# Offsets of 32 bytes between TensorE's two operands in a hybrid attention, convolution and expert block

## The chip, the cores and the metric

The kernel runs on one core of one Trainium2 chip. The metric is the device time of one execution in microseconds (us); the number given for a kernel is the median of its runs. Lower is better.

## The reference

One decoder layer on 256 tokens of width 1024, all in float32. `xn` and `hn` are RMS-normalised activations.

```
h = x + W_out( sig(g_conv) * ConformerConv(xn) + sig(g_attn) * DilatedAttn(xn) )
y = h + PEER(RMSNorm(h))

PEER, for each token and each of 8 heads:
  q = hn @ w_q                      # two halves of 128
  s = q . sub_keys                  # 128 scores per half; top 16 of each
  best 16 of the 16 x 16 sums -> experts e = i1 * 128 + i2, gate = softmax
  y += sum_e gelu(u_tab[e] . hn) * gate_e * v_tab[e]
```

There are 128 x 128 = 16,384 experts. The kernel does not gather rows: it computes the product of all of `u_tab` with all tokens, multiplies by a gate that is zero for experts not picked, and multiplies the result with all of `v_tab`.

## The kernel before

**Tiles.** Every weight arrives from HBM as a tile of 128 partitions x 1024 float32 (512 KB), through a ring of four slots, `raw`. There are 76 front tiles (projections, attention and convolution output, mixer, `w_q`), 128 tiles of `u_tab` (the key stage) and 128 of `v_tab` (the value stage). To keep float32 accuracy with the faster `float32r` matmuls, each tile is split: ScalarE writes the rounded copy `hi` (`split_hi`, L327), then VectorE or GpSimd writes the rest `lo = raw - hi` (`split_lo`, L344). Which of the two does it depends on the slot (`by_dve`): of four value tiles two go to each. Every product is then three matmuls, hi x hi, hi x lo and lo x hi, for each unit of 128 of the contraction.

**Operands.** TensorE has a stationary operand (128 columns, loaded by LDWEIGHTS, engine row PEld) and a moving operand (256 or 512 columns, streamed by MATMUL, engine row PE). In the front and key stages the stationary one is a unit of the weight tile (`hi`, `lo`), the moving one the 256 tokens. The tokens' own split parts are in `nrm` (normalised tokens, merged branches; interleaved `[k][hi, lo][256]`) or, for some jobs, in `rounded` (`xg_hi`, `xg_lo` for GLU and `w_q`; `o_hi`, `o_lo` for attention; `cu_hi`, `cu_lo` for convolution). `product` (matmul at L1222) issues these, 24 matmuls of 256 columns for a tile of the front or of the first half of the key stage. `v_tile_of` (L1322) does the v projection with `nrm` stationary and the weights moving.

**Key stage, second half.** 64 tiles go through `wide_tile`: for each of 8 units one matmul of 512 columns (`hi` with both token parts, L1478) and one of 256 (`lo` with the high part, L1480). Between them stand the matmuls of the gates (L1492, 16 to a group, one group to two tiles).

**Value stage.** `v_tile` (L1537) has the activations stationary and the value tile moving: 12 matmuls of 512 columns for a tile. The activations are in `act`; `a_split` (ScalarE, L662) and `low_part` (VectorE, L1148) write a tile's two parts into four slots of `nrm`, which the key stage no longer needs. In the first 64 value tiles VectorE also does gate work, and gate matmuls stand between tiles as before; in the last 64 there is none. The last tiles are finished at L1563 and the output is stored.

**Order.** The order on each engine is written out by hand and tied with semaphores; `pe_step` counts TensorE's steps and frees slots of `hi` and `raw`, `lo_ready` tells that a `lo` is there, `a_hi` and `a_lo` that the activations' parts are.

**Addresses.** The tensors lie one behind the other in a partition in the order of the code, every start rounded up to 32 bytes. `raw` starts at byte 16,512, a multiple of 64; `hi`, `lo` and `nrm` follow 16,384 bytes apart, and units, parts and slots are steps of 512 bytes or more, so each operand out of them starts at a multiple of 64 bytes. `rounded` starts at byte 188,448, which is 32 above a multiple of 64; so do `resid`, `qk` and `prob`, while `ident` and `act` start at multiples of 64.

The loads of the front and both halves, cut:

```
def load(src, base, it, j):
    if not (isinstance(it, int) and base + 4 * it + j < RING):
        wait_lo(sp, base - 4, it, j)
    sp.dma_start(raw[:, slot_of(base, j), :], src).then_inc(raw_in[slot_of(base, j)], 16)
```

## Time and profile before

| | before |
|---|---|
| median of 3 runs | 1028.22 us (1027.71 to 1028.9) |
| the profiled execution's own time | 1028.21 us |
| its span, first to last instruction | 1026.4 us |
| PE busy | 1020.2 us (99%) |
| VectorE, ScalarE, GpSimd busy | 811.2, 523.8, 543.4 us |
| granted TensorE clock | 1.00 (the higher level) in every slice |
| read from HBM | 180.33 MB, 179 GB/s |

The span is cut by the kernel's stages at about 225 us (mixer ends, `w_q`), 269 us (key stage), 450 us (its second half), 653 us (value stage), 850 us (its second half) and 1018 us (last sums and stores). PE's busy time says only that matmuls are always in flight: they overlap, so the pace is read from the distance between starts, not from their lengths.

### The profile page before, as it was taken

The numbers are of one execution on the slowest core, as the hardware profiler recorded it, in microseconds if no ns is written. First come the engines' busy times: TensorE is split into PE (matmuls) and PEld (weight loads), VectorE is DVE, ScalarE is ACT, GpSimd is POOL, SyncE is SP. The second block draws the span as 40 slices with busy tenths as digits, with TensorE's granted clock in tenths as the row PEclk, the third lists the DMA queues.
The fourth block names the chain that finished last, engine by engine and source line by source line (L and its number), as shares of the span: only waits on it lengthen the run. The fifth ranks groups of instructions, "written<-read, shape, count | busy, mean of one in ns | idle before, by whom it ended". The sixth has DMA issues, their size and how long they took to land.

```text
span 1026.4 us, 21174 instructions
## 1 busy us (share of the span) xinstructions
PE 1020.2 (99%) x7326; PEld 910.8 (89%) x7326; DVE 811.2 (79%) x1347; ACT 523.8 (51%) x852; POOL 543.4 (53%) x230
## 2 busy tenths in 40 slices
PE   9999999999999999999999999999999999999998
PEld 9998999999999999998888888777777778888887
DVE  6999674758799999466666666899999997677664
ACT  6553877544544444545555555544444445454553
POOL 4554455556689999864433334434443334444442
PEclk9999999999999999999999999999999999999999
DMA  6684445554455555555545555554555555655652
GB/s 242 226 289 133 138 144 182 175 178 160 146 188 182 169 192 173 184 171 174 168 163 170 177 172 176 173 176 163 165 174 172 174 173 184 201 188 186 202 191 96
DMA packets 52618, 181.93 MB, mean 177 GB/s; under 512 B 5943, under 2 KB 9155, under 8 KB 52452
## 3 DMA queue, kind: packets, MB, share of 16 engines
q1 hardware_dynamic: 52292, 181.16, 53.7%
q8 instruction: 24, 0.39, 0.2%
q10 hardware_dynamic: 288, 0.27, 0.1%
q14 instruction: 14, 0.11, 0.0%
HBM read 180.33 MB, written 3.43 MB: 179 GB/s over the span
## 4 chain that ended last, share of the span: by engine, by line
PE 96%; ACT 1%; DVE 1%; issue 1%; POOL 1%; ACTq 0%; DVEq 0%; POOLq 0%
PE bank L1222 35%; PE bank L1537 33%; PE bank L1478 12%; PE bank L1480 6%; PE bank L1492 3%; PE bank L1322 2%; PE bank L1237 1%; PE bank L1454 1%; DVE nrm L1148 1%; ACT hi L327 1%; PE bank L1246 1%; PE bank L1563 1%; PE bank L1338 0%; POOL lo L344 0%; PE bank L1361 0%
## 5 line engine op out<-in xcount | busy, mean ns | idle before, releaser
L344 POOL TENSOR_TENSOR lo<-raw,hi 128x1024 fp32r<-128x1024 f32 x216 | 540.5, 2512 | 469.0 <-ACT hi L327 468.7
L327 ACT CAST hi<-raw 128x1024 fp32r<-128x1024 f32 x332 | 347.5, 1048 | 225.0 <-PE bank L1537 191.0
L1222 PE MATMUL bank<-nrm,hi 128*128 128x256 f32 x1600 | 290.2, 284 | 0.0
L1537 PE MATMUL bank<-hi,nrm 128*128 128x512 f32 x1008 | 281.0, 395 | 1.4 <-DVE nrm L1148 1.4
L1222 PEld LDWEIGHTS bank<-nrm,hi 128*128 128x128 f32 x1600 | 249.2, 192 | 2.1 <-issue 1.3
L1222 PE MATMUL bank<-nrm,lo 128*128 128x256 f32 x800 | 226.4, 283 | 0.0
L1537 PEld LDWEIGHTS bank<-hi,nrm 128*128 128x128 f32 x1008 | 184.3, 188 | 44.9 <-DVE nrm L1148 10.0
L1148 DVE TENSOR_TENSOR nrm<-act,nrm 128x256 fp32r<-128x256 f32 x128 | 180.8, 1415 | 50.0 <-ACT nrm L662 50.0
L1478 PE MATMUL bank<-nrm,hi 128*128 128x512 f32 x512 | 181.8, 399 | 0.0
L344 DVE TENSOR_TENSOR lo<-raw,hi 128x1024 fp32r<-128x1024 f32 x116 | 148.8, 1283 | 40.2 <-ACT hi L327 40.1
L1537 PE MATMUL bank<-lo,nrm 128*128 128x512 f32 x504 | 155.8, 390 | 0.0
L1222 PEld LDWEIGHTS bank<-nrm,lo 128*128 128x128 f32 x800 | 153.3, 192 | 0.0
L1480 PE MATMUL bank<-nrm,lo 128*128 128x256 f32 x512 | 142.0, 277 | 0.0
L1478 PEld LDWEIGHTS bank<-nrm,hi 128*128 128x128 f32 x512 | 96.0, 188 | 20.9
L1537 PEld LDWEIGHTS bank<-lo,nrm 128*128 128x128 f32 x504 | 94.6, 188 | 20.3
L1480 PEld LDWEIGHTS bank<-nrm,lo 128*128 128x128 f32 x512 | 96.1, 188 | 0.0
L1222 PE MATMUL bank<-rounded,hi 128*128 128x256 f32 x496 | 89.1, 282 | 0.5 <-POOL lo L344 0.5
L1222 PEld LDWEIGHTS bank<-rounded,hi 128*128 128x128 f32 x496 | 76.2, 189 | 1.6 <-issue 0.8
L630 ACT ACTIVATE act<-bank 128x256 f32 x64 | 24.6, 384 | 93.9 <-PE bank L1222 93.8
L651 ACT COPY half_sum<-bank 128x256 f32<-128x256 f32 x64 | 23.8, 372 | 93.2 <-PE bank L1480 93.2
L1222 PE MATMUL bank<-rounded,lo 128*128 128x256 f32 x248 | 69.6, 281 | 0.0
L1154 DVE TENSOR_TENSOR half_sum<-bank,half_sum 128x256 f32<-128x256 f32 x64 | 27.0, 421 | 38.1 <-ACT half_sum L651 38.1
(188 smaller groups left out, 988.9 us busy)
## 6 DMA issues: line engine op xcount, KB each, us to landing
raw<-u_tiles SPq DMA_DIRECT2D x128, 512.0 KB, 3.3
raw<-v_tiles SPq DMA_DIRECT2D x128, 512.0 KB, 3.3
raw<-front SPq DMA_DIRECT2D x76, 512.0 KB, 3.9
toeplitz<-bias_row SPq DMA_DIRECT2D x6, 384.0 KB, 7.4
bias<-toeplitz SPq DMA_DIRECT2D x12, 128.0 KB, 3.6
resid<-x_t SPq DMA_DIRECT2D x2, 512.0 KB, 4.8
qk<-sub_keys SPq DMA_DIRECT2D x1, 1024.0 KB, 7.5
y<-act SPq DMA_DIRECT2D x3, 256.0 KB, 2.0
```

Source lines behind the costliest of these rows:

```text
L327: act_e.copy(hi[:, s, :], raw[:, s, :]).then_inc(hi_ready, 1)
L344: eng.tensor_tensor(lo[:, s, :], raw[:, s, :], hi[:, s, :].bitcast(F32), ALU.subtract)\
L630: a.activation(act[:, it * 4 + (base_i + j), :], bank[4 + j % 2][:, 0:T], ACT.Gelu).then_inc(gelu_done, 1)
L651: a.copy(half_sum[:, j % 2, :], bank[4 + j % 2][:, T:2 * T]).then_inc(crossed, 1)
L1148: dve.tensor_tensor(nrm_lo[:, s, :], act[:, it * 4 + (base_i + j), :], nrm_hi[:, s, :].bitcast(F32), ALU.subtract).then_inc(a_lo, 1)
L1154: dve.tensor_tensor(half_sum[:, j % 2, :], bank[4 + j % 2][:, 0:T], half_sum[:, j % 2, :], ALU.add)\
L1222: ins = pe.matmul(dst, w_[:, s, u * P:(u + 1) * P], x_[:, k, :], start=first and i == 0 and p_ == 0, stop=last and i == n - 1 and p_ == 2)
L1322: ins = pe.matmul(b[:, c * T:(c + 1) * T], x_[:, k, c * P:(c + 1) * P], w_[:, n % RING, 2 * m * P:2 * (m + 1) * P], start=k == 0 and c == ...
L1478: pe.matmul(b[:, :], hi[:, j, unit], nrm[:, k, :, :].rearrange("p a t -> p (a t)"), start=k == 0, stop=False, skip_group_check=True)
L1480: ins = pe.matmul(b[:, 0:T], lo[:, j, unit], nrm_hi[:, k, :], start=False, stop=k == KB - 1, skip_group_check=True)
L1492: ins = pe.matmul(bank[6 + g][:, q * HALF:(q + 1) * HALF], ohA[:, g, q // PAIR, :, q % PAIR], ohB[:, g, q // PAIR, i, :, q % PAIR], start= ...
L1537: ins = pe.matmul(bank[2 * c + half][:, :], a_[:, j, c * P:(c + 1) * P], v_[:, j, half * 512:(half + 1) * 512], start=False, stop=False, s ...
```

## The change

`SHIFT` is 8 float32, 32 bytes. Tokens (`nrm`) now start 32 bytes into their space, so that in the front and key stages the moving operand out of `nrm` starts 32 bytes above a multiple of 64, the stationary one at a multiple of 64. In the value stage the activations' parts get a view of the same space that is not shifted (`act_hi`, `act_lo`), and the value tiles' parts are written 32 bytes into their slots (`value_hi`, `value_lo`); for that the slots of `hi` and `lo` are 1040 instead of 1024 elements long. Front and key tiles still start at their slots' beginning. GpSimd's second loop over `split_lo` is cut in three, since tile 203 is the last key tile and tile 204 the first value tile. `gains` moves behind `rounded`: with 32 bytes more ahead of it and these 32 bytes less, `rounded` keeps its place 32 above a multiple of 64. `act` moves from a multiple of 64 to 32 above one. No instruction is added to or removed from a stage.

```
--- before.py
+++ after.py
@@ -42,6 +42,8 @@
 N_U = N_V = NK
 RING = 4
 LEAD = 3
+
+SHIFT = 8
 CHUNK_STEPS = PH // 2 + 9
 TOP_TILES = 48
 EXP_TILE = 52
@@ -173,10 +175,15 @@
 
 
         raw = sb("raw", [P, RING, D])
-        hi = sb("hi", [P, RING, D], F32R)
-        lo = sb("lo", [P, RING, D], F32R)
-        nrm = sb("nrm", [P, KB, 2, T], F32R)
+        hi_space = sb("hi_space", [P, RING, D + 2 * SHIFT], F32R)
+        lo_space = sb("lo_space", [P, RING, D + 2 * SHIFT], F32R)
+        hi, lo = hi_space[:, :, 0:D], lo_space[:, :, 0:D]
+        value_hi, value_lo = hi_space[:, :, SHIFT:SHIFT + D], lo_space[:, :, SHIFT:SHIFT + D]
+        norm_space = sb("norm_space", [P, KB * 2 * T + SHIFT], F32R)
+        nrm = norm_space[:, SHIFT:].rearrange("p (k a t) -> p k a t", a=2, t=T)
         nrm_hi, nrm_lo = nrm[:, :, 0, :], nrm[:, :, 1, :]
+        picked_acts = norm_space[:, 0:RING * 2 * T].rearrange("p (k a t) -> p k a t", a=2, t=T)
+        act_hi, act_lo = picked_acts[:, :, 0, :], picked_acts[:, :, 1, :]
         ident = sb("ident", [P, P])
         iota = sb("iota", [P, TOPK])
 
@@ -191,7 +198,6 @@
 
         kmask = tmp("kmask", [P, 2 * HEADS - 2])
         ksel = tmp("ksel", [HEADS, AB, P])
-        gains = tmp("gains", [P, 1])
         oneh = tmp("oneh", [BUCKETS + 1, GROUPS, BW])
         sq = tmp("sq", [P, KB, T])
         rs = tmp("rs", [P, 2, 512])
@@ -208,6 +214,7 @@
         cu_hi, cu_lo = rounded[:, 0:CB, :], rounded[:, CB:2 * CB, :]
         o_hi, o_lo = rounded[:, 2 * CB:2 * CB + AB, :], rounded[:, 2 * CB + AB:, :]
         xg_hi, xg_lo = rounded[:, 0:KB, :], rounded[:, KB:2 * KB, :]
+        gains = tmp("gains", [P, 1])
         stat = tmp("stat", [P, 16, TC * HEADS])
 
         resid = tmp("resid", [P, KB, T])
@@ -318,13 +325,17 @@
         def wait_raw(eng, base, it, j):
             eng.wait_ge(raw_in[slot_of(base, j)], uses(base, it, j) * 16)
 
+        def is_value(base, it, j):
+
+            return base + j >= V0 or isinstance(it, int) and base + 4 * it + j >= V0
+
         def split_hi(act_e, base, it, j):
 
             s = slot_of(base, j)
             wait_raw(act_e, base, it, j)
             if not (isinstance(it, int) and base + 4 * it + j < RING):
                 wait(act_e, pe_step, step_of(base - 4, it, j))
-            act_e.copy(hi[:, s, :], raw[:, s, :]).then_inc(hi_ready, 1)
+            act_e.copy((value_hi if is_value(base, it, j) else hi)[:, s, :], raw[:, s, :]).then_inc(hi_ready, 1)
 
         def by_dve(base, j):
 
@@ -341,7 +352,8 @@
 
             s = slot_of(base, j)
             eng.wait_ge(hi_ready, it * 4 + (base + j + 1))
-            eng.tensor_tensor(lo[:, s, :], raw[:, s, :], hi[:, s, :].bitcast(F32), ALU.subtract)\
+            hi_, lo_ = (value_hi, value_lo) if is_value(base, it, j) else (hi, lo)
+            eng.tensor_tensor(lo_[:, s, :], raw[:, s, :], hi_[:, s, :].bitcast(F32), ALU.subtract)\
                .then_inc(lo_ready[s], 1)
 
         def whole(k, round_):
@@ -445,11 +457,18 @@
             pool.wait_ge(normed, 2 * KB)
             pool.iota(iota_nk[:, :, :], pattern=[[1, NK], [0, PAIR]], base=0, channel_multiplier=0,
                       allow_small_or_imprecise_dtypes=True).then_inc(const, 1)
-            for base, tiles in ((U0 + LEAD, HALF), (G_SHARED, N_U + N_V - RING - HALF)):
+            for base, tiles in ((U0 + LEAD, HALF), (G_SHARED, HALF - RING)):
                 with pool.Fori(0, tiles // RING) as it:
                     for j in range(RING):
                         if not by_dve(base, j):
                             split_lo(pool, base, it, j)
+            for j in range(RING):
+                if not by_dve(G_SHARED, j):
+                    split_lo(pool, G_SHARED, HALF // RING - 1, j)
+            with pool.Fori(0, (N_V - RING) // RING) as it:
+                for j in range(RING):
+                    if not by_dve(V0 + LEAD, j):
+                        split_lo(pool, V0 + LEAD, it, j)
 
         @block.scalar
         def _(a):
@@ -659,7 +678,7 @@
             def a_split(base_i, it, j):
 
                 wait(a, pe_step, it * 4 + (S_V + base_i + j - 3))
-                a.copy(nrm_hi[:, (base_i + j) % RING, :], act[:, it * 4 + (base_i + j), :]).then_inc(a_hi, 1)
+                a.copy(act_hi[:, (base_i + j) % RING, :], act[:, it * 4 + (base_i + j), :]).then_inc(a_hi, 1)
 
             def key_round(it, first=False, last=False):
                 for j in range(RING):
@@ -1145,7 +1164,7 @@
 
                 dve.wait_ge(a_hi, it * 4 + (base_i + j + 1))
                 s = (base_i + j) % RING
-                dve.tensor_tensor(nrm_lo[:, s, :], act[:, it * 4 + (base_i + j), :], nrm_hi[:, s, :].bitcast(F32),
+                dve.tensor_tensor(act_lo[:, s, :], act[:, it * 4 + (base_i + j), :], act_hi[:, s, :].bitcast(F32),
                                   ALU.subtract).then_inc(a_lo, 1)
 
             def add_halves(it, j):
@@ -1530,8 +1549,8 @@
                 wait_lo(pe, V0 + base_i, it, j)
                 pe.wait_ge(a_hi, it * 4 + (base_i + j + 1))
                 for c in range(TC):
-                    for a_, v_ in ((nrm_hi, hi), (nrm_hi, lo), (nrm_lo, hi)):
-                        if c == 0 and a_ is nrm_lo:
+                    for a_, v_ in ((act_hi, value_hi), (act_hi, value_lo), (act_lo, value_hi)):
+                        if c == 0 and a_ is act_lo:
                             pe.wait_ge(a_lo, it * 4 + (base_i + j + 1))
                         for half in range(2):
                             ins = pe.matmul(bank[2 * c + half][:, :], a_[:, j, c * P:(c + 1) * P],
@@ -1559,9 +1578,9 @@
                     wait_lo(pe, V0 + N_V - RING, 0, j)
                     pe.wait_ge(a_hi, N_V - RING + j + 1)
                     pe.wait_ge(a_lo, N_V - RING + j + 1)
-                    for a_, v_ in ((nrm_hi, hi), (nrm_hi, lo), (nrm_lo, hi)):
+                    for a_, v_ in ((act_hi, value_hi), (act_hi, value_lo), (act_lo, value_hi)):
                         ins = pe.matmul(bank[b][:, :], a_[:, j, c * P:(c + 1) * P], v_[:, j, cols],
-                                        start=False, stop=j == RING - 1 and a_ is nrm_lo, skip_group_check=True)
+                                        start=False, stop=j == RING - 1 and a_ is act_lo, skip_group_check=True)
                 ins.then_inc(y_bank, 1)
```

## Rows read from the trace of the kernel before

**Rows 1.** The page: span, busy time, chain by engine and line.

```profile
span 1026.4 us, 21174 instructions
...
PE 1020.2 (99%) x7326; PEld 910.8 (89%) x7326; DVE 811.2 (79%) x1347; ACT 523.8 (51%) x852; POOL 543.4 (53%) x230
...
PE 96%; ACT 1%; DVE 1%; issue 1%; POOL 1%; ACTq 0%; DVEq 0%; POOLq 0%
```

**Rows 2.** The chain in order of time: start us, length us, instructions.

```profile
122.93 1.98 ACT prob L497 x8
...
159.87 39.89 PE bank L1222 x336
...
221.42 3.57 PE bank L1443 x32
225.00 37.02 PE bank L1222 x312
262.02 7.14 PE bank L1454 x64
269.16 172.85 PE bank L1222 x1440
...
849.86 168.04 PE bank L1537 x740
```

**Rows 3.** Timeline of PE in the front, three stretches: start us, length us.

```profile
28.68 0.40 PE L1222 MATMUL bank<-rounded,hi 128*128 128x256 f32 x2
...
29.39 0.40 PE L1222 MATMUL bank<-rounded,hi 128*128 128x256 f32 x2
...
32.33 0.40 PE L1222 MATMUL bank<-rounded,hi 128*128 128x256 f32 x2
...
34.49 0.40 PE L1222 MATMUL bank<-rounded,hi 128*128 128x256 f32 x2
...
161.32 0.40 PE L1222 MATMUL bank<-rounded,hi 128*128 128x256 f32 x2
...
188.07 0.40 PE L1222 MATMUL bank<-nrm,hi 128*128 128x256 f32 x2
```

**Rows 4.** The chain in order of time, second half of the key stage.

```profile
601.37 0.50 PE bank L1492 x16
...
607.50 0.50 PE bank L1492 x16
```

**Rows 5.** Timeline of PE, second half of the key stage.

```profile
461.06 0.40 PE L1478 MATMUL bank<-nrm,hi 128*128 128x512 f32 x1
...
462.45 0.40 PE L1478 MATMUL bank<-nrm,hi 128*128 128x512 f32 x1
```

**Rows 6.** Timeline of all engines, first half of the value stage.

```profile
753.72 1.06 ACT L327 CAST hi<-raw 128x1024 fp32r<-128x1024 f32 x1 [2.08 <-PE bank L1537]
...
754.86 2.52 POOL L344 TENSOR_TENSOR lo<-raw,hi 128x1024 fp32r<-128x1024 f32 x1 [3.63 <-ACT hi L327]
755.04 2.62 DVE L1148 TENSOR_TENSOR nrm<-act,nrm 128x256 fp32r<-128x256 f32 x1
...
757.71 0.77 PEld L1537 LDWEIGHTS bank<-hi,nrm 128*128 128x128 f32 x4 [0.23 <-DVE nrm L1148]
757.75 1.17 PE L1537 MATMUL bank<-hi,nrm 128*128 128x512 f32 x4
...
759.88 1.06 ACT L327 CAST hi<-raw 128x1024 fp32r<-128x1024 f32 x1 [2.07 <-PE bank L1537]
```

**Rows 7.** Waits, 653 to 850 us: total us, times, longest.

```profile
POOL lo L344 <- ACT hi L327: 117.2, 33, 3.7
...
PEld bank L1537 <- DVE nrm L1148: 9.0, 32, 0.9
```

**Rows 8.** Groups by line and shape: busy us, mean ns of one.

```profile
L1154 DVE TENSOR_TENSOR half_sum<-bank,half_sum 128x256 f32<-128x256 f32 x64 | 27.0, 421 | 38.1 <-ACT half_sum L651 38.1
...
L979 DVE TENSOR_TENSOR prob<-bank,rs 128x256 f32<-128x256 f32 x16 | 6.5, 418 | 10.3 <-PE bank L1222 10.3
```

More of the change, by code:

```diff
@@ L44 @@
 LEAD = 3
+SHIFT = 8
 CHUNK_STEPS = PH // 2 + 9
@@ L175, in hybrid_block @@
         raw = sb("raw", [P, RING, D])
-        hi = sb("hi", [P, RING, D], F32R)
-        lo = sb("lo", [P, RING, D], F32R)
-        nrm = sb("nrm", [P, KB, 2, T], F32R)
+        hi_space = sb("hi_space", [P, RING, D + 2 * SHIFT], F32R)
+        lo_space = sb("lo_space", [P, RING, D + 2 * SHIFT], F32R)
+        hi, lo = hi_space[:, :, 0:D], lo_space[:, :, 0:D]
+        value_hi, value_lo = hi_space[:, :, SHIFT:SHIFT + D], lo_space[:, :, SHIFT:SHIFT + D]
+        norm_space = sb("norm_space", [P, KB * 2 * T + SHIFT], F32R)
+        nrm = norm_space[:, SHIFT:].rearrange("p (k a t) -> p k a t", a=2, t=T)
         nrm_hi, nrm_lo = nrm[:, :, 0, :], nrm[:, :, 1, :]
+        picked_acts = norm_space[:, 0:RING * 2 * T].rearrange("p (k a t) -> p k a t", a=2, t=T)
+        act_hi, act_lo = picked_acts[:, :, 0, :], picked_acts[:, :, 1, :]
         ident = sb("ident", [P, P])
@@ L193, in hybrid_block @@
         ksel = tmp("ksel", [HEADS, AB, P])
-        gains = tmp("gains", [P, 1])
         oneh = tmp("oneh", [BUCKETS + 1, GROUPS, BW])
@@ L210, in hybrid_block @@
         xg_hi, xg_lo = rounded[:, 0:KB, :], rounded[:, KB:2 * KB, :]
+        gains = tmp("gains", [P, 1])
         stat = tmp("stat", [P, 16, TC * HEADS])
@@ L319, in wait_raw, with is_value @@
             eng.wait_ge(raw_in[slot_of(base, j)], uses(base, it, j) * 16)
+        def is_value(base, it, j):
+            return base + j >= V0 or isinstance(it, int) and base + 4 * it + j >= V0
         def split_hi(act_e, base, it, j):
@@ L326, in split_hi @@
                 wait(act_e, pe_step, step_of(base - 4, it, j))
-            act_e.copy(hi[:, s, :], raw[:, s, :]).then_inc(hi_ready, 1)
+            act_e.copy((value_hi if is_value(base, it, j) else hi)[:, s, :], raw[:, s, :]).then_inc(hi_ready, 1)
         def by_dve(base, j):
@@ L343, in split_lo @@
             eng.wait_ge(hi_ready, it * 4 + (base + j + 1))
-            eng.tensor_tensor(lo[:, s, :], raw[:, s, :], hi[:, s, :].bitcast(F32), ALU.subtract)\
+            hi_, lo_ = (value_hi, value_lo) if is_value(base, it, j) else (hi, lo)
+            eng.tensor_tensor(lo_[:, s, :], raw[:, s, :], hi_[:, s, :].bitcast(F32), ALU.subtract)\
                .then_inc(lo_ready[s], 1)
@@ L447, in _ @@
                       allow_small_or_imprecise_dtypes=True).then_inc(const, 1)
-            for base, tiles in ((U0 + LEAD, HALF), (G_SHARED, N_U + N_V - RING - HALF)):
+            for base, tiles in ((U0 + LEAD, HALF), (G_SHARED, HALF - RING)):
                 with pool.Fori(0, tiles // RING) as it:
@@ L452, in _ @@
                             split_lo(pool, base, it, j)
+            for j in range(RING):
+                if not by_dve(G_SHARED, j):
+                    split_lo(pool, G_SHARED, HALF // RING - 1, j)
+            with pool.Fori(0, (N_V - RING) // RING) as it:
+                for j in range(RING):
+                    if not by_dve(V0 + LEAD, j):
+                        split_lo(pool, V0 + LEAD, it, j)
         @block.scalar
@@ L1532, in v_tile @@
                 for c in range(TC):
-                    for a_, v_ in ((nrm_hi, hi), (nrm_hi, lo), (nrm_lo, hi)):
-                        if c == 0 and a_ is nrm_lo:
+                    for a_, v_ in ((act_hi, value_hi), (act_hi, value_lo), (act_lo, value_hi)):
+                        if c == 0 and a_ is act_lo:
                             pe.wait_ge(a_lo, it * 4 + (base_i + j + 1))
@@ L1561, in _ @@
                     pe.wait_ge(a_lo, N_V - RING + j + 1)
-                    for a_, v_ in ((nrm_hi, hi), (nrm_hi, lo), (nrm_lo, hi)):
+                    for a_, v_ in ((act_hi, value_hi), (act_hi, value_lo), (act_lo, value_hi)):
                         ins = pe.matmul(bank[b][:, :], a_[:, j, c * P:(c + 1) * P], v_[:, j, cols],
-                                        start=False, stop=j == RING - 1 and a_ is nrm_lo, skip_group_check=True)
+                                        start=False, stop=j == RING - 1 and a_ is act_lo, skip_group_check=True)
                 ins.then_inc(y_bank, 1)
```

4 lines of the change are left out of this document (2 added, 2 removed).

## The prediction

> **What bounds the kernel.** I read the page first: PE is busy for 1020.2 of 1026.4 us, and 96% of the chain that ended last is PE [rows 1]. No other engine ends more than 1% of it. So the time is the number of matmuls times their pace, and the question is what a 32-byte offset does to the pace. Busy time can't tell, since matmuls overlap; the chain in order of time can. In the first half of the key stage 1440 matmuls of 256 columns take 172.85 us, 120.0 ns each, with no wait between them. In the second half of the value stage 740 matmuls of 512 columns take 168.04 us, 227.1 ns, or 226.7 without the wait of 0.3 us at their start [rows 2]. The clock is at 2.4 GHz throughout, so these are 288 and 544 cycles: 32 more than columns in both. Those 32 cycles per matmul, whatever the number of columns, are the only thing that the change can touch. With some 5,100 matmuls out of `nrm` they are about 68 us of the time.
>
> **A comparison the kernel already holds.** Jobs at the same line, of the same size, take their moving operand either from `nrm` (a multiple of 64 bytes, like the weights) or from `rounded` (32 above one, while the weights are at 0). This is just the relation that the change gives to `nrm`. The `w_q` tiles, from `rounded`: 312 matmuls in 37.02 us, 118.65 ns [rows 2]. Attention and convolution, from `rounded`: 240 matmuls between 159.87, where the chain's piece starts, and 188.07, where the first `nrm` matmul starts [rows 2, 3]; 28.20 / 240 is 117.5 ns, with a restart at its beginning that makes the pace itself about 117.1. The other 96 of that piece of 336, mixer tiles from `nrm`, take the rest, 159.87 + 39.89 - 188.07 = 11.69 us, 121.8 ns with the end of the group. But a third stretch of `rounded`, the GLU tile after the bias rows, has 18 matmuls from 32.33 to 34.49: 120.0 ns. The tile before the bias rows had 6 from 28.68 to 29.39, 118.3 ns [rows 3]. So at an offset of 0 the pace is 120.0 wherever I look, and at 32 it settles, according to how the group was entered, on 117.1, 118.65 or 120.0. The gain of the offset is 0 to 2.9 ns a matmul. By number of matmuls (240 at 117.1, some 500 at 118.65, one or two tiles at 120.0) the middle one is the commonest; I take 118.65, a gain of 1.35 ns.
>
> **The parts of the change.**
>
> 1. *Key stage, first half.* 64 tiles x 24 = 1536 matmuls of 256 columns, all on the path. 1536 x 1.35 = 2.1 us; bounds 0 and 1536 x 2.9 = 4.5.
>
> 2. *Front tiles out of `nrm`.* 12 q/k, 16 gate and 8 mixer tiles at L1222 and 6 v tiles at L1322 are 42 x 24 = 1008 matmuls. Not all are on the path: from 122.93 on, for some 12 us, the chain runs through ScalarE, its exponentials first [rows 2], which is about 100 matmuls' time. So 900 count: 1.2 us; bounds 0 and 2.6. These are short groups between other work, which must be entered anew each time.
>
> 3. *Key stage, second half.* A pair of 512 and 256 columns takes 348 ns (four from 461.06 to 462.45 [rows 5]), 67 cycles above its 768 columns, again some 32 for each. There is no wait: 16 pairs of 348 ns and a gate group of 0.50 us make 6.07 of the 6.13 us between two gate groups [rows 4]. 1024 matmuls x 1.35 = 1.4 us; but two lengths alternate here, no row shows them at an offset of 32, and I take 1.0; bounds 0 and 3.0.
>
> 4. *Value stage, second half.* The two operands change roles: activations stationary at 0, values moving at 32. 768 matmuls of 512 columns. As the surplus of 32 cycles is the same for 512 as for 256 columns, I carry the gain over: 1.0 us; bounds 0 and 2.2.
>
> 5. *Value stage, first half.* Here a faster PE isn't worth its whole gain. VectorE's `low_part` starts at 755.04 and needs 2.62 us, because it stands until GpSimd's subtraction, begun at 754.86, is over (2.52 us); PE's weight load then ends a wait of 0.23 us, at 757.71. The next `split_hi` starts at 759.88, when PE has finished that tile, and 759.88 - 753.72 = 6.16 us is the period of two tiles [rows 6]. So this is a closed loop: ScalarE 1.06, GpSimd 2.52, VectorE's rest about 0.3, and 2.13 us of PE, from 757.75 to 759.88. PE is in it with 8 of the 24 matmuls. The wait shows in all periods: 32 times, 9.0 us in all [rows 7]. The gain is 256 matmuls x 1.35 = 0.35 us, and the other 512 only make PE wait longer. Upper bound: 256 x 2.9 = 0.7. If the loop were broken it would be three times as much.
>
> 6. *Splits and copies at a new offset.* `split_hi` and `split_lo` write value parts at 32 from a source at 0, and `act` moves by 32. VectorE's rows at both offsets agree: 256 columns to `prob`, at 32, take 418 ns, to `half_sum`, at 0, 421 [rows 8]. I take 0, for ScalarE too, since `split_hi` waits for PE in any case (2.08 us before it [rows 6]). GpSimd has no row at 32, see the rivals. In the second half of the value stage GpSimd waits for most of its time, so an increase of less than a microsecond there is hidden.
>
> 7. *GpSimd's loop in three pieces* issues the same subtractions: it has 117.2 us of waits in 33 pieces in the stage that follows [rows 7], 3.6 us each, which hide some more branches. If they fell into the loop of part 5 it would be once, well under 1 us. The DMAs write the same addresses of `raw`, and nothing new is queued on SP. The move of `gains` leaves `rounded` at 32, so GLU, attention, convolution and `w_q` keep their relation: 0. Their entry, though, can change, by at most the 1.5 ns between two of the paces above for 744 matmuls, 1.1 us either way.
>
> Sum: 2.1 + 1.2 + 1.0 + 1.0 + 0.35 = 5.65 us off the profiled execution's 1028.21 us (1.8 us more than its span, and equal to the median of 1028.22 within 0.01), so 1022.5 us. With all at the best pace seen: 4.5 + 2.6 + 3.0 + 2.2 + 0.7 = 13.0, so 1015.2. With all at 120.0: 1028.2.
>
> A page speaks against the whole gain. Beside the rows of [rows 2, 3], where equal matmuls run at 117.1 to 120.0 ns, stands the rule of the Trainium skill, "SBUF — State Buffer", section "Who interferes with whom": TensorE has two independent read ports, one for the moving operand and one for LDWEIGHTS, and never waits on anyone. If so, no placement of one against the other can matter, and the time stays 1028.2. The trace bears that out only for true float32 matmuls: 32 transposing ones with `ident` at 0 and `resid` at 32 take 3.57 us, 64 with both at 32 take 7.14 us, 111.6 ns in both cases [rows 2].
>
> **The rivals.**
>
> *The offset isn't what makes `rounded` faster.* `rounded` lies 120 KB above the weights, with its high and low parts 8 KB apart instead of interleaved. If one of these made the difference, `nrm` at 32 would stay at 120.0: 1028.2 us. For it: one stretch of `rounded` ran at 120.0 [rows 3], and the float32 rows don't know the offset [rows 2]. Against: 552 or more matmuls did run faster, and no stretch from `nrm` did. The same time comes out if the long groups happen to settle on 120.0.
>
> *All stages settle on the fast pace*, as attention and convolution did for 28 us: 1015 to 1019 us. For it: the pace once taken is held for whole groups, and the first half of the key stage is one group of 1536, so that its whole term is won or lost at its entry. Against: 312 matmuls of `w_q`, just ahead of it and the closest in form, held 118.65.
>
> *The 32 cycles are mostly a collision that the offset removes*, and `rounded` is held up by something else. Then the gain could be several times larger: at the shortest distances inside these groups, about 115 ns, some 5 ns x 4,500 is 22 us, 1006. No stretch kept such a pace; small.
>
> *GpSimd gets slower on value tiles (the other side).* Its subtraction of value tiles now reads `raw` at 0 and `hi` at 32 and writes at 32. It is in the loop of part 5, so each 0.1 us more costs 32 x 0.1 = 3.2 us, and VectorE, shut out meanwhile, passes it on to PE in full. From 0.18 us more (7% of 2.52) it outweighs the 5.65 us; with 0.4 us it is 1028.2 + 12.8 - 5.65 = 1035. For it: nothing in the trace shows GpSimd at mixed offsets. Against: VectorE's equal rows at both [rows 8].
>
> **How the numbers follow.** Gain as forecast, 3 to 9 us: 0.45. Fast pace nearly everywhere, 9 to 14 us: 0.18. More than the rows show: 0.07. No effect beyond 2 us: 0.21. Slower through GpSimd or a worse pace: 0.09. This measurement tells apart changes of about 0.2%, 2 us. Forecast 1022.5. The range of 1014.5 to 1028.8 holds the first two cases, and most of the no-effect one, about 0.82. The likeliest case alone has 1019 to 1025. Faster 0.70, same 0.21, slower 0.09.
>
> **What would show it right or wrong.** In the chain the piece of 1440 matmuls at L1222 shortens from 172.85 us to about 170.9 (at 117.1 ns: 168.6), the 740 at L1537 from 168.0 to about 167. The period of the wide tiles goes from 6.13 to about 6.10, the period in the first half of the value stage from 6.16 to 6.15 with a longer wait of PE for VectorE. ScalarE, VectorE and GpSimd keep their means for L327, L344 and L1148. If the pace is 120.0 everywhere the offset was not the cause; if L344 on GpSimd is above 2.6 us the other side is right; if the value stage moves and the key stage doesn't, roles or lengths of the operands matter and my carrying over from 256 to 512 columns was wrong.

## The result: slower by 0.4%, and the profile after

The changed kernel takes 1032.22 us, the kernel before 1028.04 in the same comparison (6 runs each): ratio 1.004, 95% interval [1.0029, 1.0051]. I had forecast 1022.5 us, 0.55% faster.

The page of the changed kernel still shows a kernel of matmuls:

```profile
span 1030.6 us, 21171 instructions
...
PE 1024.4 (99%) x7326; PEld 911.5 (88%) x7326; DVE 808.2 (78%) x1347; ACT 523.2 (51%) x852; POOL 551.0 (53%) x230
```

Its chain in order of time (start us, length us, instructions) answers to [rows 2]; L1241 is the L1222 of before, L1556 the L1537:

```profile
224.43 36.95 PE bank L1241 x312
...
268.51 170.63 PE bank L1241 x1440
...
848.78 173.14 PE bank L1556 x740
```

The first half of the key stage did what I forecast: 1440 matmuls in 170.63 instead of 172.85 us, 118.5 ns instead of 120.0. The second half of the value stage did the opposite: 740 matmuls in 173.14 instead of 168.04 us, 234.0 instead of 227.1 ns with the wait at their start.

The first gate group of each stage marks its beginning, and gate group 64 the end of the mixed part of the value stage. Timeline of PE, before:

```profile
454.01 0.66 PE L1492 MATMUL bank<-ohB,ohA 128*128 128x64 f16 x16
...
650.27 0.66 PE L1492 MATMUL bank<-ohB,ohA 128*128 128x64 f16 x16
...
842.32 0.66 PE L1492 MATMUL bank<-ohB,ohA 128*128 128x64 f16 x16
```

and after:

```profile
451.01 0.66 PE L1511 MATMUL bank<-ohB,ohA 128*128 128x64 f16 x16
...
648.44 0.66 PE L1511 MATMUL bank<-ohB,ohA 128*128 128x64 f16 x16
...
841.30 0.66 PE L1511 MATMUL bank<-ohB,ohA 128*128 128x64 f16 x16
```

| stage | before us | after us | difference | forecast |
|---|---|---|---|---|
| front, up to 269.16 / 268.51 | 269.16 | 268.51 | -0.65 | -1.2 |
| key stage, first half | 184.85 | 182.50 | -2.35 | -2.1 |
| key stage, second half | 196.26 | 197.43 | +1.17 | -1.0 |
| value stage, first half | 192.05 | 192.86 | +0.81 | -0.35 |
| value stage, second half and end | 184.1 | 189.3 | +5.2 | -1.0 |
| sum | 1026.4 | 1030.6 | +4.2 | -5.65 |

So most of the loss is in matmuls of 512 columns, and the question is what made them slower: the offset itself, the roles of the two operands in the value stage, or the longer slots that the offset needed.

### The profile page after: what moved, and what is told of

The parts are those of the page before. It is cut to its first block, busy times and chain, and to the rows that moved or that the text cites. A ratio compares the mean times of both kernels' runs of the same rounds, so it can differ in the third digit from the quotient of the medians.

```text
span 1030.6 us, 21171 instructions
## 1 busy us (share of the span) xinstructions
PE 1024.4 (99%) x7326; PEld 911.5 (88%) x7326; DVE 808.2 (78%) x1347; ACT 523.2 (51%) x852; POOL 551.0 (53%) x230
## 4 chain that ended last, share of the span: by engine, by line
PE 96%; ACT 2%; DVE 1%; issue 1%; POOL 1%; ACTq 0%; DVEq 0%; POOLq 0%
PE bank L1241 34%; PE bank L1556 34%; PE bank L1497 12%; PE bank L1499 6%; PE bank L1511 3%; PE bank L1341 2%; PE bank L1256 1%; PE bank L1473 1%; DVE norm_space L1167 1%; ACT hi_space L338 1%; PE bank L1265 1%; PE bank L1582 1%; PE bank L1357 0%; POOL lo_space L356 0%; PE bank L1380 0%
## 5 line engine op out<-in xcount | busy, mean ns | idle before, releaser
L356 POOL TENSOR_TENSOR lo_space<-raw,hi_space 128x1024 fp32r<-128x1024 f32 x216 | 548.1, 2548 | 465.1 <-ACT hi_space L338 464.5
L338 ACT CAST hi_space<-raw 128x1024 fp32r<-128x1024 f32 x332 | 346.7, 1045 | 229.8 <-PE bank L1556 197.0
L1241 PE MATMUL bank<-norm_space,hi_space 128*128 128x256 f32 x1600 | 286.6, 282 | 0.0
L1556 PE MATMUL bank<-hi_space,norm_space 128*128 128x512 f32 x1008 | 284.2, 398 | 1.1 <-DVE norm_space L1167 1.1
L1241 PEld LDWEIGHTS bank<-norm_space,hi_space 128*128 128x128 f32 x1600 | 245.2, 188 | 2.2 <-issue 1.5
L1556 PEld LDWEIGHTS bank<-hi_space,norm_space 128*128 128x128 f32 x1008 | 186.7, 188 | 45.3 <-DVE norm_space L1167 2.4
L1241 PE MATMUL bank<-norm_space,lo_space 128*128 128x256 f32 x800 | 224.4, 280 | 0.0
L1497 PE MATMUL bank<-norm_space,hi_space 128*128 128x512 f32 x512 | 183.0, 398 | 0.0
L1556 PE MATMUL bank<-lo_space,norm_space 128*128 128x512 f32 x504 | 158.3, 395 | 0.0
L1241 PEld LDWEIGHTS bank<-norm_space,lo_space 128*128 128x128 f32 x800 | 151.0, 189 | 0.0
L1499 PE MATMUL bank<-norm_space,lo_space 128*128 128x256 f32 x512 | 143.4, 280 | 0.0
L1556 PEld LDWEIGHTS bank<-lo_space,norm_space 128*128 128x128 f32 x504 | 94.6, 188 | 22.9
L1497 PEld LDWEIGHTS bank<-norm_space,hi_space 128*128 128x128 f32 x512 | 96.1, 188 | 20.7
L1499 PEld LDWEIGHTS bank<-norm_space,lo_space 128*128 128x128 f32 x512 | 96.5, 189 | 0.0
L1241 PE MATMUL bank<-rounded,hi_space 128*128 128x256 f32 x496 | 89.1, 282 | 0.6 <-POOL lo_space L356 0.6
L1241 PEld LDWEIGHTS bank<-rounded,hi_space 128*128 128x128 f32 x496 | 76.1, 188 | 1.8 <-POOL lo_space L356 0.8
L1241 PE MATMUL bank<-rounded,lo_space 128*128 128x256 f32 x248 | 69.5, 280 | 0.0
```

Source lines behind the costliest of these rows:

```text
L338: act_e.copy((value_hi if is_value(base, it, j) else hi)[:, s, :], raw[:, s, :]).then_inc(hi_ready, 1)
L356: eng.tensor_tensor(lo_[:, s, :], raw[:, s, :], hi_[:, s, :].bitcast(F32), ALU.subtract)\
L1241: ins = pe.matmul(dst, w_[:, s, u * P:(u + 1) * P], x_[:, k, :], start=first and i == 0 and p_ == 0, stop=last and i == n - 1 and p_ == 2)
L1497: pe.matmul(b[:, :], hi[:, j, unit], nrm[:, k, :, :].rearrange("p a t -> p (a t)"), start=k == 0, stop=False, skip_group_check=True)
L1499: ins = pe.matmul(b[:, 0:T], lo[:, j, unit], nrm_hi[:, k, :], start=False, stop=k == KB - 1, skip_group_check=True)
L1556: ins = pe.matmul(bank[2 * c + half][:, :], a_[:, j, c * P:(c + 1) * P], v_[:, j, half * 512:(half + 1) * 512], start=False, stop=False, s ...
```

## The experiments

Twelve runs take the change apart, two more follow up a surprise. Where a kernel has a ratio, it is to the kernel before on the same chip; the chips of experiments 1 to 3, 4 and 5, 9 to 11, and 13 and 14 differ, so across these sets the ratios compare and the medians only roughly. The groups of matmuls alone (experiments 6, 7, 8 and 12) ran once each. "Distance" is from here on the start of the moving operand less that of the stationary one, as a remainder after whole blocks of 256 bytes; why 256 is the outcome of these runs.

**1. Values back at 0, slots still long.**

```
-        value_hi, value_lo = hi_space[:, :, SHIFT:SHIFT + D], lo_space[:, :, SHIFT:SHIFT + D]
+        value_hi, value_lo = hi, lo
```

> The changed kernel with the value tiles' parts written at the start of their long slots again (tokens still at 32, activations at 0, slots still 1040 elements). By length (an offset of 32 bytes between the operands helps matmuls of 256 columns and harms those of 512): the last 64 value tiles go back from 233.6 to 226.7 ns a matmul, the gate periods of the first 64 from 6.17 to about 6.15, the total from 1032.2 to about 1026.2. By slot spacing (slots 64 bytes longer spoil the relation of value parts and activations): the pace stays near 233.6 and the total near 1032.

Measured: 1029.89 us, ratio 1.0015 [1.0006, 1.0024]. The chain has

```profile
268.45 170.62 PE bank L1241 x1440
...
848.15 171.28 PE bank L1556 x740
```

The value stage's second half gets back 1.86 of 5.10 us; its pace, without the wait of 0.3 us at the start, is 231.1 ns, neither forecast. Both theories as I had put them fall: the offset costs something, and the 3.24 us that are left came with the long slots.

**2. Both operands of the value stage at 32.**

```
-        picked_acts = norm_space[:, 0:RING * 2 * T]
+        picked_acts = norm_space[:, SHIFT:SHIFT + RING * 2 * T]
```

> The changed kernel with the value stage's activations 32 bytes above a multiple of 64 as well, so that both operands there have the same offset and neither is at 0. If the distance between the operands decides: 226.7 ns in the last 64 value tiles, about 1026.2 in all. If it is the moving operand's own start off a multiple of 64 that costs: 233.6 ns and 1032. Slot spacing would also leave it at 233.6.

Measured: 1029.89 us, ratio 1.0014 [1.0005, 1.0023].

```profile
847.99 171.32 PE bank L1556 x740
```

The same 231.1 ns as in the first, and again neither forecast. Both operands 32 bytes on cost the same as both at 0, so here their distance counts and not where they start.

**3. Tokens alone, short slots.** Experiment 1 with slots of 1024 elements:

```
-        hi_space = sb("hi_space", [P, RING, D + 2 * SHIFT], F32R)
+        hi_space = sb("hi_space", [P, RING, D], F32R)       # and lo_space
```

> Only the tokens moved by 32 bytes: slots of 1024 elements, value parts and activations at 0. By length: first half of the key stage 118.5 ns, its second half still with gate periods of 6.17 us (its 512-column matmuls lose what the 256-column ones win), last 64 value tiles 226.7 ns, total about 1026.2. If slot spacing took part, the second half of the key stage goes back to 6.13 and the total to about 1025.

Measured: 1022.86 us, ratio 0.9943 [0.993, 0.9957], 0.6% faster than before.

```profile
603.53 0.50 PE bank L1511 x16
609.66 0.50 PE bank L1511 x16
...
845.79 168.03 PE bank L1556 x740
```

The gate groups of the second half of the key stage are 6.13 us apart again (6.17 in the changed kernel and in experiment 1), as in the second branch, and the value stage has its 168.03 us. The total is 2 us below that branch; about half of it is the first half of the key stage, which ran at 117.8 ns and not at 118.5. The 64 bytes between the slots were worth 7.0 us of median (1029.89 less 1022.86), and 5.8 us between the two profiled executions: 0.75 before the second half of the key stage, 1.4 in it, 0.3 in the first half of the value stage and 3.4 behind. Of the 4.1 us that this profiled execution (1024.14 us, the slowest of five) gains on the kernel before, 3.8 lie ahead of the second half of the key stage.

**4. Slots alone.** The kernel before with slots of 1040 elements and no offset anywhere:

```
-        hi = sb("hi", [P, RING, D], F32R)
+        hi_space = sb("hi_space", [P, RING, D + 16], F32R)   # and lo, lo_space
+        hi, lo = hi_space[:, :, 0:D], lo_space[:, :, 0:D]
```

> The kernel before with slots of 1040 elements and nothing shifted, so that every distance is a multiple of 64 bytes but not of 512. If the distance counts within 512 bytes: last 64 value tiles 231.1 ns as in the run with the values back at 0, first half of the key stage off 120.0 (117.8 to 119), second half of the key stage near 6.17, total 1028.2 + 3.4 + 0.5 to 1.3 less 1 to 2.5, about 1030. If it counts within 64 bytes: 120.0 and 226.7 ns, 1028.2.

Measured: 1029.75 us, ratio 1.0021 [1.0011, 1.003].

```profile
269.00 170.66 PE bank L1223 x1440
...
848.95 171.28 PE bank L1538 x740
```

With no operand of these stages off a multiple of 64 bytes, the first half of the key stage gains as much as in the changed kernel (118.5 ns) and the value stage loses as in experiment 1, as the first branch said. So the remainder modulo 64, by which the prediction had sorted the operands, is not the one that counts. GpSimd's loop is in its old pieces here, so their division is no part of the value stage's loss either.

**5. The offset in the value stage without long slots.** Experiment 3, with the activations' slots 32 bytes on:

```
-        picked_acts = norm_space[:, 0:RING * 2 * T]
+        picked_acts = norm_space[:, SHIFT:SHIFT + RING * 2 * T]
```

> Tokens and the value stage's activations both 32 bytes on, slots short, value parts at 0: the distance of 32 bytes of the changed kernel in the value stage without its long slots. If 32 bytes spoil matmuls of 512 columns by themselves: 233.3 ns in the last 64 value tiles and about 1022.9 + 5.2 = 1028 or a little more. If only the long slots did it: 226.7 ns and 1022.9.

Measured: 1028.63 us, ratio 1.0011 [1.0001, 1.0021].

```profile
845.33 172.94 PE bank L1556 x740
```

The offset by itself, now with the other operand moved (a distance of -32, which is 224), gives 233.3 ns in the value stage, 4.9 us more than in experiment 3 and 0.7% of ratio, as the first branch said.

The run shows one thing more. In the first half of the key stage every operand lies where it lay in experiment 3, at a distance of 32, and yet the pace differs. Windows of the matmuls at L1241, experiment 3 and then this one (stretch, its length, PE's busy time with the count):

```profile
280.00:400.00 120.00, 120.00 (x1022) 120.00 (x1021) 1.00 0.56 185
```

```profile
280.00:400.00 120.00, 120.00 (x1031) 120.00 (x1030) 1.00 0.56 185
```

The stretch and one matmul's own 0.28 us, by the count, is 117.7 and 116.7 ns. Up to there the two programs do the same work at the same addresses; they ran on different chips. So a distance does not fix one pace; it has a few, and which one a group takes is not decided by the addresses alone.

**6. Groups of matmuls alone.** To have the rule without the kernel, groups of 96 matmuls with a weight load each, nothing else running; the loop, its two numbers of columns written as one, is

```
for i in range(96):
    pe.matmul(bank[..][:, 0:n], w[:, i % 8 * P:i % 8 * P + P],
              m[:, off // 4 + i % 2 * n:off // 4 + i % 2 * n + n], ...)   # n = 256, 512
```

> No reference computation: it leaves out everything but groups of 96 float32r matmuls, each with its own weight load, at distances of 0, 16, 32, 48, 64 and 96 bytes between the operands' places in a block of 64 bytes, at 256 and at 512 columns, three times over. By length: 120.0 and 226.7 ns at 0 and 64, about 118.5 and 233.6 at 32 and 96. By the role of the operands (weights or activations stationary) or by what other engines do at the time: 512 columns at 32 are not slower here than at 0. 16 and 48 have no forecast; between the two if the effect grows with the distance, near one of them if it is a matter of hit or miss.

The six moving tensors of this first one lay at different distances beside their nominal offset (0, 144, 32, 176, 64 and 224 modulo 256), which I had not taken into account. At 0 it gave 120.0 and 226.7 ns each time; at the distance of 32 it gave 116.7 and 233.3. So 512 columns at 32 are slower with nothing else running, and the other engines are no part of it. The expected 120.0 and 226.7 at the nominal 64 (a real 64) did not come: 117.8 three times, and 228.9, 233.3 and 228.9.

**7. Exact distances within 512 bytes**, one pair of tensors:

> No reference computation: only groups of 96 matmuls, at 256 and at 512 columns, with one pair of tensors and exact distances within 512 bytes of 0, 16, 32, 64, 96, 128, 192, 256, 320, 384, 448 and 480, up and then down. Distance within 512 bytes: 120.0 and 226.7 only at 0, elsewhere 116.6 to 119.3 and mostly 233.3, with something between at 64. Distance within 64 bytes: 120.0 and 226.7 again at 64, 128, 192 and so on.

Timeline of PE, one window inside a group each (start us, length us, count of matmuls). At 256 columns, for the distances 32, 64 and 256 in this order, and then at 512 columns for 0, 32 and 256:

```profile
29.72 8.45 PE L194 MATMUL bank<-mm,w 128*128 128x256 f32 x71
...
40.78 8.44 PE L194 MATMUL bank<-mm,w 128*128 128x256 f32 x73
...
85.80 8.44 PE L194 MATMUL bank<-mm,w 128*128 128x256 f32 x69
...
142.82 18.53 PE L198 MATMUL bank<-mm,w 128*128 128x512 f32 x81
...
186.64 18.59 PE L198 MATMUL bank<-mm,w 128*128 128x512 f32 x79
...
298.66 18.52 PE L198 MATMUL bank<-mm,w 128*128 128x512 f32 x81
```

The pace is the length less one matmul's own 0.28 us (0.39 at 512 columns), by the count less one: 8.44 - 0.28 over 68 is 120.0 ns at 256, 8.44 - 0.28 over 72 is 113.3 at 64; 18.59 - 0.39 over 78 is 233.3 at 32, 18.52 - 0.39 over 80 is 226.6 at 256. All groups, up and down:

| distance | 256 columns, ns | 512 columns, ns |
|---|---|---|
| 0 and 256 | 120.0 | 226.7 |
| 16 | 118.7, 116.7 | 231.7 |
| 32 | 116.7 | 233.3 |
| 64 and 320 | 113.3, 117.8 | 228.9 |
| 96 | 120.0 | 233.4 |
| 128 and 384 | 118.7 | 233.3, 232.4 |
| 192 and 448 | 117.8, 113.3 | 233.3 |
| 480 | 118.3 | 233.3 |

256 repeats 0, and 320, 384 and 448 give no pace that 64, 128 and 192 don't. Within these 512 bytes the period is 256, finer than the 512 I had said and coarser than the 64 of the prediction. A distance of 0 is the best place for 512 columns and nearly the worst for 256. At 16, 64 and 192 there are two paces at 256 columns: 192, for instance, took 117.8 ns behind the group at 128 and 113.3 behind the one at 256. What chooses between them is not shown.

With this the long slots can be added up, since each next slot lies 64 bytes further. In experiments 1, 2 and 4 the value parts are at 0, 64, 128 and 192 in turn; the mean of 226.7, 228.9, 233.3 and 233.3 is 230.6 ns, against the 231.1 measured. In the changed kernel they are at 32, 96, 160 and 224, none of which is fast: 233.6 there, and 233.3 or 233.4 alone (160 was not tried; 144 and 176 gave 233.3 in experiment 6). In the first half of its key stage the four distances are 32, 224, 160 and 96, which take 116.7, 118.3, 117.3 and 120.0 ns alone (the second and third in experiment 12); the mean is 118.1, against 118.5.

**8. Other numbers of columns**, at distances 0 and 32:

> No reference computation: groups of 96 matmuls of 64 to 512 columns in steps of 64, at distances of 0 and of 32 bytes. If at 0 the surplus is a fixed 32 cycles and elsewhere it grows with the columns (about 26 at 256, 48 at 512), the two cross near 320 columns: at 384 it is 416 cycles (173.3 ns) against about 420 (175).

Timeline of PE as above; 192 columns at 0 and at 32, 384 at 0 and at 32, and for the second time over 256 at 32, 448 at 32 and 448 at 0:

```profile
88.76 6.41 PE L194 MATMUL bank<-mm,w 128*128 128x192 f32 x46
...
102.82 6.41 PE L194 MATMUL bank<-mm,w 128*128 128x192 f32 x56
...
163.73 11.60 PE L194 MATMUL bank<-mm,w 128*128 128x384 f32 x66
178.81 13.51 PE L194 MATMUL bank<-mm,w 128*128 128x384 f32 x77
...
380.33 9.88 PE L194 MATMUL bank<-mm,w 128*128 128x256 f32 x81
...
464.70 18.56 PE L194 MATMUL bank<-mm,w 128*128 128x448 f32 x89
...
484.73 17.59 PE L194 MATMUL bank<-mm,w 128*128 128x448 f32 x86
```

192 columns: 111.7 ns at both distances. (The first of these rows has fewer matmuls because its first ones, up to 91 us, are still 213 ns apart; see the last section.) 320: 146.7 at both. 384: 173.3 at both. 448: 206.7 and then 202.7 at 0, 204.5 and then 206.7 at 32. 512: 226.7 against 233.3. My picture of a surplus that grows evenly with the columns and crosses the 32 cycles near 320 is wrong: at 320 and 384 the two are equal, at 448 neither is reliably the faster, at 512 a distance of 0 is. There is no straight line to carry a price along. And 256 columns at 32 took 117.8 ns the first time and 120.0 the second, as slow as at 0, where experiment 7 had 116.7 both times. The two halves of the moving tensor are 2048 bytes apart here and 1024 there, and other groups go before; these runs do not tell which of the two matters.

**9 to 11. Tokens at 192 and at 64 bytes** in the whole kernel (short slots, values and activations at 0):

```
-SHIFT = 8
+SHIFT = 48        # tokens_at_192; 16 in tokens_at_64
```

> As tokens_only, but with the tokens 192 bytes on instead of 32 (values and activations at 0, short slots); rounded comes to 64 bytes from the weights modulo 256. The distance counts modulo 256, and 192 gave 113.3 ns or 117.8 at 256 columns in the groups run alone, by the way the group was entered. If the key stage's first half locks on 113.3: 2400 matmuls x 6.7 ns less than before, 16 us, and up to 4 more from rounded, about 1010. If on 117.8: 5.4 us less, about 1022.5. If the distance counted only modulo 64, as the prediction had it, 192 would be 0: 120.0 ns, 1028.

> The same with 64 bytes; rounded comes to 192 modulo 256. Same two paces as for 192, 113.3 or 117.8, so about 1010 or 1022.5; modulo 64 it would be 1028.

> tokens_at_192 with 128 bytes of padding ahead of rounded, so that rounded is at 192 as well. It tells whether rounded's 744 matmuls follow the same rule as nrm's: within 1 us of tokens_at_192 if both distances lock alike, up to 3.3 us away if one locks on 113.3 and the other on 117.8.

Measured: 1023.31 us, ratio 0.996 [0.9946, 0.9974]; 1024.14 us, ratio 0.996 [0.9945, 0.9975]; 1023.10 us, ratio 0.9952 [0.9937, 0.9967]. The first half of the key stage did lock on 113.3 ns in all three, for which about 1010 us was forecast, and still nothing was gained over experiment 3; the totals near 1022.5 are those of the other branch, by another mechanism. In the profiled execution of tokens_at_192 the second half of the key stage begins 2.6 us earlier than in experiment 3 and takes 2.9 us more. The waits of tokens_at_192 between 262 and 450 us, and PE's windows there (stretch, its length and PE's busy time, granted clock, DMA):

```profile
PE bank L1241 <- ACT act L649: 3.5, 1, 3.5
```

```profile
380.00:410.00 30.00, 30.00 (x267) 1.00 0.60 201
410.00:420.00 10.00, 6.50 (x44) 0.80 0.16 53
420.00:436.00 16.00, 16.00 (x132) 0.91 0.58 199
```

PE has caught up with VectorE's search for the top 16: ScalarE waits for its end to take the gates' exponential, at key tile 52, with the next GELU behind it in its queue, and PE waits 3.5 us for that GELU. The granted clock is then 0.80 and 0.91 in the two stretches, after an idle PE, and the matmuls from 417 to 423 us are 213 ns apart. Further on, the second half of the key stage has a period of 6.22 us at 192:

```profile
603.21 0.50 PE bank L1511 x16
609.42 0.50 PE bank L1511 x16
```

and 6.23 at 64, against 6.13: 32 times 0.09 is 2.9 us. In `w_q`, `rounded` took 118.0 ns at 64 (tokens_at_192) and 114.8 at 192 (the other two).

**12. The pairs of the second half of the key stage, alone.**

> No reference computation: 48 pairs of a 512-column and a 256-column matmul, and then 96 of 256 columns, at distances of 0 to 224 bytes in steps of 32, up and down. The pairs as in the second half of the key stage: 345 ns at 0 as there; at 32 the same, since that stage kept its period of 6.13 us in tokens_only; longer at those distances that the long slots brought in, 96, 160 or 224, where it had 6.17. The 256-column groups, entered from another form each time, show whether 64 and 192 hold 113.3 ns or depend on the entry.

The chain shows each group of 48 pairs (L194) and the 96 matmuls of 256 columns behind it (L196); here for 32 and 64 going up, the pairs of 96, and for 0 at the very end:

```profile
34.84 16.65 PE bank L194 x96
51.48 11.20 PE bank L196 x96
62.68 16.75 PE bank L194 x96
79.43 11.30 PE bank L196 x96
90.74 16.81 PE bank L194 x96
...
428.29 16.65 PE bank L194 x96
```

A pair takes 346.7 ns at 32, 160 and 224, 350 at 96, 351 at 128, 353 at 192, 349 or 353 at 64, 353 or 347 at 0 (345 was forecast for 0 and 32). Of the three distances expected to be longer, only 96 is. These paces fit the lack of a loss at 32 and the loss at 192 and 64 in the kernel; of the long slots (32, 224, 160 and 96 in turn) only one slot in four shows it here, a quarter of 3.3 ns x 16 pairs = 0.013 us, against 0.04 us measured. The rest of those 1.2 us is not accounted for.

**13. The exponential four tiles later**, on top of tokens_at_192:

```
-EXP_TILE = 52
+EXP_TILE = 56
```

> tokens_at_192 with the exponential of the gates, for which ScalarE waits for VectorE's top 16, four key tiles later. If that wait was where the gain went, the first half of the key stage takes 1536 x 113.3 = 174 us without a wait and with full clock, 5 to 6 us less than in tokens_at_192: about 1018. If VectorE's top 16 still ends last, at the transposes before tile 60, some of the wait moves there and the total stays at 1021 to 1023.

Measured: 1023.64 us, ratio 0.9952 [0.9939, 0.9966], no gain. The first half of the key stage up to tile 60 does take 164.5 instead of 169.8 us, but the waits now show

```profile
PE bank L1511 <- DVE ohB L1148: 2.8, 1, 2.8
```

VectorE has to build the first gates between tile 60 and the second half. GpSimd's subtractions are back to back by then (eight in 19.74 us from 425.38 on), and beside them VectorE's operations on the gates take 2.5 to 2.9 us each; the same ones take 0.4 to 0.7 us as soon as they are over. The wait moved, as the second branch said, but to the gates and not to the transposes, where it is still VectorE that waits for PE (7.7 us); the total is a little above that branch's 1021 to 1023.

**14. Each stage at its own distance.** late_exp, with the parts of all tiles from the second half of the key stage on written 192 bytes further, in slots 4096 bytes apart, and `rounded` at 192; the loops of ScalarE and GpSimd are divided where the place changes. The main lines of the edit:

```
+        late_hi, late_lo = [x[:, SHIFT:SHIFT + RING * D].rearrange("p (s d) -> p s d", d=D)
+                            for x in (hi_space, lo_space)]
-        picked_acts = norm_space[:, 0:RING * 2 * T]
+        picked_acts = norm_space[:, SHIFT:SHIFT + RING * 2 * T]
...
+                first_late = isinstance(it, int) and LATE <= base + 4 * it + j < LATE + 3
+                wait(act_e, pe_step, step_of(base - 4 + first_late, it, j))
```

> late_exp with each stage at its own distance: front and first half of the key stage at 192 (113.3 ns at 256 columns), and from the second half of the key stage on weights, values and activations written 192 bytes further as well, so that their distance is 0 (226.7 ns at 512 columns); slots keep a spacing of 4096 bytes, and for that the first three such tiles wait for one tile more; rounded at 192. If distance modulo 256 is the whole matter: gate periods of the second half of the key stage back from 6.22 to 6.13 (2.8 us), value stage as before, w_q near 114.8, so about 4 us below late_exp, 1014. If the longer wait at the change of place costs, it shows as a wait of PE between the halves of the key stage, 1 to 3 us.

Measured: 1016.12 us, ratio 0.9883 [0.9868, 0.9898]: 1.2% faster than the kernel before, 1.6% than the changed one.

```profile
600.60 0.50 PE bank L1515 x16
606.73 0.50 PE bank L1515 x16
...
837.54 168.07 PE bank L1560 x740
```

The period is 6.13 us again and the value stage at 168.07. It is 7.5 us below late_exp and not the 4 forecast, mainly because the 2.8 us wait is gone as well: `split_hi` waits one tile longer for the first shifted tiles, which leaves GpSimd idle from 435.5 to 436.9 us, and in that time VectorE's operations on the first gates take 0.4 to 0.7 us each. The first half of the value stage, though, has a period of 6.17 us here against 6.15 in late_exp; that was not forecast and is not explained.

## Why the prediction was wrong

**The step that failed** is in part 4: "As the surplus of 32 cycles is the same for 512 as for 256 columns, I carry the gain over". At 512 columns a distance of 0 is the best place, with 32 surplus cycles, and 32 bytes have 48 (233.3 ns, experiments 5 to 7). This term was forecast at -1.0 and measured +5.2 us, which is 6.2 of the 9.9 us between the forecast and the measured sum. The trace had no row of 512 columns at any other distance, and I bounded the term by 0 and 2.2 us of gain from rows of another length, with no end on the side of a loss. The upper end of the range, 1028.8, hung on that bound.

**The comparison under it was the wrong one too.** "This is just the relation that the change gives to `nrm`" took the remainder modulo 64. What counts is the remainder modulo 256 (experiments 4 and 7). There `rounded` is at 160 from the weights, and `nrm` in the changed kernel at 32, 224, 160 or 96, by the slot, since slots of 4160 bytes shift it by 64 each. That the forecast of 118.65 ns came out at 118.5 is luck in part: at 256 columns most distances other than 0 cost 116.7 to 120.0, and the slots went through four of them.

**Part by part.** Part 1, -2.1 forecast, -2.35 measured: the size is right and the reason is not, since the long slots alone, with no offset, gave the same 118.5 ns (experiment 4). Part 2, -1.2 forecast, -0.65 measured; the first product started 0.6 us later after a longer warm-up (its 54 matmuls 8.54 instead of 7.72 us), which leaves a gain of 1.25 for the rest, near the forecast. No run separates the tiles out of `nrm` in it. Part 3, -1.0 forecast, +1.17 measured: the wrong sign, and not by the offset but by the slots, since with short ones the period is 6.13 (experiment 3); even there nothing was gained, because a pair takes 346.7 ns at 32 and at the faster of its two paces at 0 (experiment 12). I had copied the slots' length into the front and given it no term. Part 5, -0.35 forecast, +0.81 measured: the closed loop was read rightly for the kernel before, but matmuls of about 234 ns broke it in the unforeseen direction. In the changed kernel, between 653 and 850 us, the wait of [rows 7] is nearly gone:

```profile
POOL lo_space L356 <- ACT hi_space L338: 108.0, 32, 3.8
...
PEld bank L1556 <- DVE norm_space L1167: 1.4, 2, 0.8
```

and PE alone sets the period, 6.17 us. The slack of 0.23 us per two tiles, which I had counted only as a limit to a gain, also took up most of the loss: 24 matmuls slower by 6.6 ns each would be 0.16 us a period, and it grew by 0.03.

Parts 6 and 7, 0 forecast. GpSimd's `split_lo` went from 2541 to 2738 ns in that stage:

```profile
L356 POOL TENSOR_TENSOR lo_space<-raw,hi_space 128x1024 fp32r<-128x1024 f32 x32 | 87.6, 2738 | 108.0 <-ACT hi_space L338 108.0
```

By my own sign ("above 2.6 us the other side is right") that would confirm the rival that GpSimd suffers from mixed offsets. It doesn't: in experiment 2, where the value parts are written at 32 as in the changed kernel, it has 2532 ns, and in experiment 5, with value parts at 0, 2737:

```profile
L356 POOL TENSOR_TENSOR lo_space<-raw,hi_space 128x1024 fp32r<-128x1024 f32 x29 | 73.4, 2532 | 105.0 <-ACT hi_space L338 105.0
```

(experiment 2, 660 to 835 us). In the second half of the value stage, at the same offsets, the changed kernel has 2408 against 2394 before. The long operations come in the two kernels where PE alone sets the period of that stage; what lengthens them is not shown, and almost nothing waits for them. The sign was badly chosen.

**The rivals.** That the offset has no effect is wrong, for the key stage already (experiment 3). That all stages take the fast pace is wrong by experiment 7 for 512 columns. The rule cited from "SBUF — State Buffer", section "Who interferes with whom" of the Trainium skill, that TensorE's two read ports are independent and that it never waits on anyone, would leave no room for the distance, and these runs do not agree with that: with all other engines idle and nothing changed but the distance, matmuls of 512 columns took 226.7 to 233.4 ns and those of 256 from 113.3 to 120.0. The measurement decides. Whether the two reads meet in the memory or somewhere else on the way is not shown; no run tells that apart.

**The other side**, the slower kernel that came, had 0.09 for GpSimd "or a worse pace"; the mechanism and the price were written out for GpSimd alone, where it isn't. A rival "at 512 columns the present distance is the good one" would have been as open as the gain: the trace held no matmul of 512 columns at any other distance.

## What to carry to other kernels

For float32r matmuls with a weight load each, the distance in bytes between stationary and moving operand modulo 256 moved the pace by up to 3% at 512 columns and 6% at 256, and a distance can have more than one pace: look at it for every stage by itself, by its number of columns, measure it in place, and see to it that slots, padding and rounding of sizes keep it. When a row of another size is all there is, its price holds for that size; bound the unseen case on both sides of zero. And before a faster stage is worth anything, find who arrives next: here the top 16 on VectorE stood 20 us ahead of PE at the transposes (VectorE waited 20.1 us for PE there), but its consumer on ScalarE eight tiles before had nothing to spare, and waited 1.1 us for it in experiment 3 and 4.0 in tokens_at_192.

## What the hardware showed that I had not expected

- One group of matmuls holds its pace to about 1 ns, and the same distance can hold several: at 256 columns 113.3 or 117.8 ns at 64 and 192 bytes, and 116.7, 117.8 or 120.0 at 32; at 512 columns 228.9 or 233.3 at 64. No run shows what chooses; experiments 3 and 5 already differ where their programs are still the same.
- Below 256 columns the columns stop mattering: 192 columns took 111.7 ns, and 64 columns as much while the clock was at its higher level, in the first 4 us of the second pass of experiment 8.
- In the groups of 64 and 128 columns the granted clock fell to 0.50, the lower level, with PE busy throughout by its records, in that second pass; they were then 213 ns apart:

```profile
236.00:276.00 40.00, 40.00 (x175) 32.62 (x174) 0.00 (x0) 0.00 (x0) 1.00 0.00 1
...
300.00:330.00 30.00, 30.00 (x142) 30.00 (x142) 0.00 (x0) 0.00 (x0) 0.50 0.00 1
```

(windows: PE's and the weight loads' busy time with counts, ScalarE, GpSimd, granted clock, DMA). The first pass has the same 213 ns in its groups of 64 and 128 columns, from 4 to 91 us, though its rows give 1.00 there, as

```profile
45.00:85.00 40.00, 40.00 (x189) 40.00 (x189) 0.00 (x0) 0.00 (x0) 1.00 0.00 1
```

So the distance between starts has to be read beside the clock column, at the start of a program above all.
